# The stored activations of the 256-column stages start 64 bytes earlier in their rows

## The reference

```python
for layer in range(DEPTH):                       # first block
    h = h + (rglru_mixer | nsa_mixer)(rmsnorm(h, g[layer]), ...)
    h = h + conv_ffn(rmsnorm(h, ffn_norm_g[layer]), ...)
x = rmsnorm(h, final_norm_g)
for l in range(DEPTH):                           # second block
    h  = modulate(rmsnorm_2(x,  norm1_g[l]), sh1, sc1)
    hc = modulate(rmsnorm_2(xc, norm1_g[l]), csh1, csc1)
    a, naq, nak, nav, gq, gk, gv, gates = split_in(h @ w_in[l])
    ...
    x = x + g1 * merge(br_a, br_b, br_c, gates, w_out[l])
    x = x + g2 * swiglu(modulate(rmsnorm_2(x, norm2_g[l]), sh2, sc2), w_ffn_in[l], w_ffn_out[l])
```

## The kernel before

| stages | moving operand | floats from the row's start | start, bytes past a multiple of 256 |
|---|---|---|---|
| first block, layer 1 of the second | h, 256 tokens (512 for gkv1, nak1) | 48 | 64 |
| layer 0 of the second | h, 512 tokens | 0 | 128 |
| feed-forward out, 256 tokens | hid | 0 | 64 |
| feed-forward out, 512 tokens | hid | 16 | 128 |
| nsa_v, nav0, nav1 | w, 512 columns | | 128 |

## Time and profile before

### The profile page before, as it was taken

The page is one execution under the profiler, slowest core; times in us unless marked ns, Lnnn a source line. Parts: engine busy times, 40 slices in busy tenths (PEclk is TensorE's granted clock), DMA queues, the critical chain, the costliest instruction groups (busy, mean ns, idle before and its releaser), DMA issues.

```text
span 2217.5 us, 33708 instructions
## 1 busy us (share of the span) xinstructions
PE 2062.2 (93%) x12860; PEld 1769.9 (80%) x12860; DVE 1531.4 (69%) x2851; ACT 842.3 (38%) x1337; POOL 385.4 (17%) x342
## 2 busy tenths in 40 slices
PE   6899999879999799988899999999997898999998
PEld 6799999748999678746576578888887875999998
DVE  7668899395889669876887873274367867446554
ACT  4633444273344332375311232222223337524443
POOL 0003324002334510000000032200233000003322
PEclk9999999889999799999999989999998999999999
DMA  6355566304556422101455532243243320435552
GB/s 236 120 190 190 189 244 213 144 1 165 184 182 247 153 84 96 57 1 73 174 211 192 194 133 95 95 171 133 97 151 141 133 77 1 153 149 187 197 190 95
DMA packets 46988, 318.10 MB, mean 143 GB/s; under 512 B 5008, under 2 KB 8080, under 8 KB 9488
## 3 DMA queue, kind: packets, MB, share of 16 engines
q1 hardware_dynamic: 45568, 309.58, 38.2%
q0 software_dynamic: 1296, 6.82, 0.8%
HBM read 315.33 MB, written 1.05 MB: 143 GB/s over the span
## 4 chain that ended last, share of the span: by engine, by line
PE 57%; DVE 29%; ACT 5%; issue 5%; DMA 3%; POOL 1%; DVEq 1%; SPq 0%; ACTq 0%; POOLq 0%
PE ps L625 54%; DVE w_lo L1491 8%; DVE ps L1511 8%; ACT arena L1116 3%; DMA ring<-wstream 2%; PE ps L870 2%; DVE arena L1647 1%; DVE arena L1645 1%; DVE small L1689 1%; ACT w_hi L1116 1%; DVE ps L1643 1%; DVE arena L1709 1%; DVE ps L1656 1%; DVE ps L1678 1%; DVE arena L1861 1%
## 5 line engine op out<-in xcount | busy, mean ns | idle before, releaser
L625 PE MATMUL ps<-h_hi,w_hi 128*128 128x256 f32 (+1 forms) x2616 | 837.8, 320 | 37.5 <-DVE h_lo L1478 12.4
L625 PE MATMUL ps<-h_lo,w_hi 128*128 128x256 f32 (+1 forms) x2616 | 824.6, 315 | 0.0
L625 PE MATMUL ps<-h_hi,w_lo 128*128 128x256 f32 (+1 forms) x2616 | 823.7, 315 | 0.0
L1491 DVE TENSOR_TENSOR w_lo<-ring,w_hi 128x1024 fp32r<-128x1024 f32 x433 | 554.8, 1291 | 359.5 <-ACT w_hi L1116 358.6
L1116 ACT ACTIVATE w_hi<-ring 128x1024 fp32r<-128x1024 f32 x433 | 448.5, 1054 | 543.1 <-PE ps L625 431.1
L625 PEld LDWEIGHTS ps<-h_hi,w_hi 128*128 128x128 f32 x2616 | 497.5, 190 | 82.0 <-issue 21.9
L625 PEld LDWEIGHTS ps<-h_lo,w_hi 128*128 128x128 f32 x2616 | 497.8, 190 | 33.9 <-issue 1.2
L625 PEld LDWEIGHTS ps<-h_hi,w_lo 128*128 128x128 f32 x2616 | 497.6, 190 | 33.0
L1116 ACT ACTIVATE arena<-ps 128x512 f32<-128x512 f32 (+2 forms) x246 | 140.9, 575 | 455.4 <-PE ps L625 409.9
L1511 DVE SCALAR_TENSOR_TENSOR ps<-ring,arena 128x512 f32<-128x512 f32 x384 | 269.3, 780 | 0.0
L625 PE MATMUL ps<-arena,ring 128*128 128x256 f32 (+2 forms) x840 | 217.8, 420 | 21.2 <-DMA ring<-wstream 7.6
(11 more groups left out here) (177 smaller groups left out, 1753.4 us busy)
## 6 DMA issues: line engine op xcount, KB each, us to landing
ring<-wstream SPq DMA_DIRECT2D x290, 1024.0 KB, 4.8
arena<-c_in POOLq DMA_DIRECT2D x7, 512.0 KB, 4.5
arena<-rpb POOLq DMA_DIRECT2D x2, 1536.0 KB, 8.5
x<-x_in SPq DMA_DIRECT2D x2, 1024.0 KB, 12.2
out<-arena SPq DMA_DIRECT2D x8, 128.0 KB, 2.0
cst<-consts SPq DMA_DIRECT2D x1, 928.0 KB, 11.9
prm<-params SPq DMA_DIRECT2D x1, 580.0 KB, 10.6
ring<-wstream SPq DMA_DIRECT2D x1, 512.0 KB, 3.6
```

Source lines behind the costliest of these rows:

```text
L625: ins = nc.tensor.matmul(*a, **k)
L1491: V.tensor_tensor(w_lo[:, job % SPLITS, :], raw_job(job), w_hi[:, job % SPLITS, :].bitcast(F32), ALU.subtract).then_inc(weights_ready, 1)
```

## The change

One number: the 256-token view of h_hi and h_lo starts at float 32 (128 bytes) of the row instead of float 48 (192 bytes). All its readers and writers go with it. No instruction is added, taken away or moved on any engine. h of the 256-token stages now starts at a multiple of 256 bytes: h_hi at 98560, h_lo at 115456. The 512-token view, the weights and hid stay.

```diff
-        h_at = {n: [v[:, at:at + KD * S2].rearrange("p (k t) -> p k t", t=S2) for v in h_rows] for n, at in ((S, 48), (S2, 0))}
+        h_at = {n: [v[:, at:at + KD * S2].rearrange("p (k t) -> p k t", t=S2) for v in h_rows] for n, at in ((S, 32), (S2, 0))}
```

## The result

| | before | after |
|---|---|---|
| median, us (runs) | 2226.85 (5) | 2234.91 (5) |
| lowest to highest | 2223.77 to 2228.97 | 2231.73 to 2237.79 |
| profiled execution / its span | 2219.34 / 2217.5 | 2231.73 / 2229.9 |

The changed kernel is slower: ratio 1.0037, 95% interval 1.0023 to 1.0052, +8.1 us between the medians. The forecast was no measurable difference, 2228 us.

What follows compares the result with a forecast made beforehand. The chain of waits ran 57% through TensorE and 29% through VectorE, with TensorE at 97.7% in layer 1's tail. Profiled 2219.3 + 0 - 0.5 = 2218.8, plus 9.0 to the median, gave 2228 us, range 2217 to 2243.

Steps and rivals of the forecast that it cites:

- term 2: 256-column matmuls on the chain (layer 1 tail and input projections, sparse attention's projections): taken as 0, bounded -2.9 to +7.1 us.
- Term 1: 256-column matmuls of lru_in, ffn_in0 and ffn_in1, where something else sets the pace: cost 0 between 113 and 117.6 ns.
- Term 3: 512-column matmuls on the 256-token view (gkv1, nak1, nav1, nsa_v): from -1.0 to 0 us, taken as -0.5 us.
- Terms 4 and 5: VectorE's writing of h_lo is indifferent to placement, 0; hid, weights and x stay, and hid keeps both rhythms.
- the longer rhythm: Rival: 256-column matmuls slow to 122.2 ns, on the chain and where the cover is gone; 2258 us, chance 0.05.
- all slow: Rival: all groups fall into the slow 117.6 ns rhythm, in the whole tail of layer 1; +6.6 us, 2235 us, chance 0.25.

## Why the prediction was wrong

The step that failed is term 2, "I take 0: the choice of rhythm changes from unit to unit of one loop at one address, so chance or the moment of the start decides much of it". Something that the placement does not fix, and that no run names, does choose between two rhythms, in the changed kernel too. But which rhythms there are to choose from is set by D: 113.3 and 117.7 ns at D = 192, 118.5 and 120.0 at D = 128. The term took a property of one placement for a property of the matmul. The bound failed with it: +7.1 us came from the two rhythms seen, 113.0 and 117.6. With the new mean of 119.1 the term is, by the same weights, 2194 x 6.1 - 641 x 4.6 = 10.4 us. Measured were 8.1 us between medians; in the profiles the tail of layer 1 alone, for which these weights give about 8 us (1782 x 6.1 - 563 x 4.6), takes 8.1 more.

Term 1, weights by stage: the 0 for ffn_in0 and ffn_in1 was nearly right, its limit was not. The prediction has the cover used up at 117.6 ns and 2.8 us lost for each further nanosecond; at 120.0 ns in ffn_in1 VectorE kept its time to 0.1 us in 113. For the stages apart: a matmul of layer 1 cost 7.6 us / 2208, 3.4 ns, one of the first block 3.3 us over some 3200, 1.0 ns, with an interval from 0 to 2.1.

Term 3, -0.5 us: wrong in sign. The 512-column products wanted the weights' own start, D = 0, which the change does not give (D = 128). nak1 stayed at 233, nav1 lost 4 ns each, 96 of them 0.4 us. The rows for it were there: nak1 slow with h at 64 and w at 128, nav1 slower than nav0 with the roles exchanged. I took the start on a multiple of 128 for what was common to the fast ones, and named the difference of starts only as an argument within a rival. That the start decides "in the 512-column products always, not now and then" is also too strong: nav1 with one placement had 229.3 and 231.2 ns in different runs.

Terms 4 and 5 (writers, hid): right, 479 ns, and hid keeps both rhythms.

The rival that happened is the longer rhythm, with the size of "all slow": every group slow, 119.1 ns, 2235 us. I gave the two together 0.30. That the time is just the price of "all slow" is luck: that price stands on 117.6 ns and on a gain at 512 columns, and neither came. The rule of the Trainium skill ("SBUF — State Buffer", section "Who interferes with whom": two independent read ports for the moving operand and the weight load) would have the two starts independent of each other. The runs disagree: the spacing at 512 columns goes from 226.9 to 232.9 ns when only the weights are moved. They do not tell whether it is the port or something behind it.

## What to carry to other kernels

Where one-pass float32 matmuls stand back to back and set the pace, the starts of the two operands modulo 256 bytes are worth a sweep, 226.9 to 233 ns at 512 columns and 114.5 to 120 at 256. Sweep for each number of columns by itself: the best difference for one is the worst for the other. And a mix of two rhythms at one placement is no evidence about another placement; bound an untried one by more than the rhythms seen, and say which pair of addresses each row compares.

## What was not expected of the hardware

Equal starts are the best at 512 columns (226.9 ns) and the worst at 256 (119.9). The effect has a sign: D = 64 and D = 192 are 229.0 and 233.3 ns at 512 columns, 117.7 and 114.5 at 256. Moving one of the two weight buffers by 64 bytes cost 21 us in the execution seen (2244.9 against 2223.8), more than any move of h: at 256 columns it gave 118.2 ns on h and 118.3 on hid, though two thirds of the matmuls kept their D of 192.

At one placement the rhythm is a choice between two, and the placement sets which two: 113.3 and 117.7 ns with D = 192, 118.5 and 120.0 with D = 128.
